# Expert rows of a sparse transformer block: stored by token through a scatter instead of by slot

## The reference, cut to what matters

```python
def hier_moe(h, ...):                       # h: (1024 tokens, 1024)
    ...                                     # group by softmax, then top 2 of its 8 experts
    experts = grp[:, None] * EXPERTS_PER_GROUP + top_i          # 2 experts a token
    dest = pstarts[e_s] + (jnp.arange(A) - starts[e_s])         # slots, padded to 128 an expert
    x_buf = zeros((P, D)).at[dest].set(tok[t_s])
    def run(xb, e):
        return (silu(xb @ w_gate[e]) * (xb @ w_up[e])) @ w_down[e]
    out = zeros((N, D)).at[t_buf].add(y_buf * w_buf[:, None])
x = x + gt2 * hier_moe(h, ...)
return rmsnorm(x, g_norm_final)
```

## Time and profile before

| what | value |
|---|---|
| median of 3 runs | 1641.82 us (1639.29 to 1643.68) |
| the profiled execution's own time | 1644.57 us |
| its span, first to last instruction | 1642.6 us |
| PE, DVE, ACT, POOL busy | 89%, 69%, 55%, 16% of the span |
| mean granted PE clock | 0.941 |
| stores of Y, `y_dram<-WK` on ACT's queue | 32 of 512 KB |
| clearing, `y_dram<-zero` on ACT's queue | 8 of 3072 KB |
| row gathers, `WK<-xn_dram,gidx` on POOL | 32 |
| last gathers, `BIG<-y_dram,srow` on POOL | 16 |

### The profile page before, as it was taken

One profiled execution on the slowest core, in us unless ns is written; L12 is line 12 of the kernel. 1 busy time (PEld: TensorE's weight loads), 2 busy tenths in 40 slices (PEclk: granted clock), 3 DMA queues, 4 the chain that ended last, 5 costly groups with the idle time before them and its releaser, 6 DMA issues.

```text
span 1642.6 us, 21585 instructions
## 1 busy us (share of the span) xinstructions
PE 1463.9 (89%) x7420; PEld 1137.6 (69%) x7420; DVE 1125.4 (69%) x1511; ACT 908.8 (55%) x1223; POOL 265.0 (16%) x191
## 2 busy tenths in 40 slices
PE   3899999999999899788899965999999999999960
PEld 2587345888887787455666654888888888888850
DVE  6632698672247994433444366999999999999947
ACT  5321577878995111423444414777777777777732
POOL 0000110240001001200000001332232232232105
PEclk9899899999999989589999986999999999999985
DMA  9198643213234233311111117999999999999957
GB/s 370 63 338 316 213 157 110 88 69 111 105 117 132 67 128 134 120 51 65 65 57 47 45 52 265 378 396 404 406 400 398 397 396 396 399 399 398 393 212 303
DMA packets 102566, 368.01 MB, mean 224 GB/s; under 512 B 11232, under 2 KB 23648, under 8 KB 77792
## 3 DMA queue, kind: packets, MB, share of 16 engines
q1 hardware_dynamic: 74208, 291.58, 46.6%
q10 hardware_dynamic: 17024, 41.95, 6.7%
q0 software_dynamic: 11264, 33.57, 5.5%
HBM read 306.24 MB, written 69.21 MB: 229 GB/s over the span
## 4 chain that ended last, share of the span: by engine, by line
PE 74%; DVE 14%; ACT 4%; issue 3%; DMA 2%; POOL 2%; SPq 0%; DVEq 0%; POOLq 0%; ACTq 0%
PE PS L1633 19%; PE PS L1635 19%; PE PS L1634 19%; PE PS L1734 3%; PE PS L1757 2%; PE PS L1956 2%; PE PS L1844 2%; PE PS L1831 1%; DVE wlo L1486 1%; DVE WK L1045 1%; DMA WK<-in_w_ada 1%; PE PS L1690 1%; POOL BIG L731 1%; PE PS L1719 1%; PE PS L1931 1%
## 5 line engine op out<-in xcount | busy, mean ns | idle before, releaser
L1486 DVE TENSOR_TENSOR wlo<-raw,whi 128x2048 fp32r<-128x2048 f32 x192 | 436.2, 2287 | 37.9 <-ACT whi L956 35.0
L956 ACT ACTIVATE whi<-raw 128x2048 fp32r<-128x2048 f32 x192 | 364.0, 1913 | 126.6 <-DVE WK L1569 80.8
L1633 PE MATMUL PS<-whi,xhi 128*128 128x512 f32 x512 | 203.9, 398 | 4.4 <-DVE xlo L1556 3.2
L1635 PE MATMUL PS<-whi,xlo 128*128 128x512 f32 x512 | 201.1, 393 | 0.0
L1634 PE MATMUL PS<-wlo,xhi 128*128 128x512 f32 x512 | 200.1, 391 | 0.0
L838 ACT ACTIVATE KV<-ACC,WK 128x1024 int8<-128x1024 f32 (+4 forms) x160 | 147.5, 925 | 23.8 <-DVE WK L1181 21.1
L1633 PE MATMUL PS<-KVR,BIGR 128*128 128x512 f32 x320 | 126.9, 397 | 1.1 <-ACT WK L823 1.1
L1635 PE MATMUL PS<-KVR,BIGR 128*128 128x512 f32 x320 | 124.9, 390 | 0.0
L1634 PE MATMUL PS<-KVR,BIGR 128*128 128x512 f32 x320 | 124.5, 389 | 0.0
L695 POOL COPY wcol<-tw 128x1 f32 (+1 forms) x32 | 63.0, 1970 | 370.1 <-DVE WK L1587 370.1
L1633 PEld LDWEIGHTS PS<-whi,xhi 128*128 128x128 f32 x512 | 97.0, 189 | 24.7 <-DVE xlo L1556 4.0
(11 more groups left out here) (329 smaller groups left out, 2907.3 us busy)
## 6 DMA issues: line engine op xcount, KB each, us to landing
raw<-in_w_gate SPq DMA_DIRECT2D x64, 1024.0 KB, 7.1
raw<-in_w_up SPq DMA_DIRECT2D x64, 1024.0 KB, 7.8
raw<-in_w_down SPq DMA_DIRECT2D x64, 1024.0 KB, 7.3
y_dram<-zero ACTq DMA_DIRECT2D x8, 3072.0 KB, 11.3
WK<-in_w_ada POOLq DMA_DIRECT2D x16, 1024.0 KB, 7.4
y_dram<-WK ACTq DMA_DIRECT2D x32, 512.0 KB, 7.1
KV<-in_w_in SPq DMA_DIRECT2D x5, 2048.0 KB, 10.2
KV<-in_x SPq DMA_DIRECT2D x16, 512.0 KB, 4.9
```

What stands on the lines that cost most here:

```text
L956: nc.scalar.activation(whi[:, slot], raw[:, q], ACT.Copy).then_inc(G("m_hi"), 1)
L1486: V.tensor_tensor(wlo[:, slot], raw[:, q], whi[:, slot].bitcast(F32), ALU.subtract)\
L1633: mm(out_, x_hi, w_hi, start=first, stop=False)
L1635: return mm(out_, x_lo, w_hi, start=False, stop=final)
```

## The change

`y_dram` becomes 2048 rows: row t holds the result of token t from one of its experts, row 1024 + t that of the other. The half is chosen in routing: the pair with the higher slot number of a token's two goes to the upper half (`at`). The table now holds the destination row (token, or 1024 + token), and serves for both directions: `xn_dram` is stored twice, one copy behind the other, so that gathering by it works too. The store from ACT is gone; POOL scatters Y by an indirect DMA that skips empty slots, one item later in its own program. The clearing is gone. At the end SP loads both halves with plain DMAs. The lower rows (y1) are complete when the last item but one has been scattered (`m_end` 1), so their loads run beside the last item's down product; DVE adds them after the last Y, and the upper rows (y2) after that. The remainder of the first gate half is made after the table instead of before it, and in the last step the remainders of the down halves are made before `h`.

```diff
-        xn_dram = nc.dram_tensor("xn_dram", (S, D), F32).ap()
-        y_dram = nc.dram_tensor("y_dram", (MAX_ITEMS * P, D), F32).ap()
+        xn_dram = nc.dram_tensor("xn_dram", (2 * S, D), F32).ap()
+        y_dram = nc.dram_tensor("y_dram", (2 * S, D), F32).ap()
...
@@ sync
-                    sp.dma_start(xn_dram[tile(TILES[i - 1]), :], WC["sq"]).then_inc(G("st_xn"), 16)
+                    for half in range(2):
+                        sp.dma_start(xn_dram[tile(T * half + TILES[i - 1]), :], WC["sq"]).then_inc(G("st_xn"), 16)
...
             sp.wait_ge(G("m_end"), 1)
-            sp.dma_start(WF["x"][T - 1], x1_dram[tile(T - 1), :]).then_inc(G(f"ld_x{T - 1}"), 16)
+            for t in range(T):
+                sp.dma_start(WF["y1"][t], y_dram[tile(t), :]).then_inc(G(f"f_y{t}"), 16)
+            sp.wait_ge(G("m_end"), 2)
+            sp.wait_ge(G("st_y1"), 8 * count(rounds))
+            for t in range(T):
+                sp.wait_ge(G(f"f_y{t}"), 16)
+                sp.dma_start(WF["y2"][t], y_dram[tile(T + t), :]).then_inc(G(f"f_y{t}"), 16)
...
@@ gpsimd
+            def scatter(s):
+                nc.gpsimd.indirect_dma_start(
+                    out=y_dram, out_offset=bass.IndirectOffsetOnAxis(ap=gidx[:, 2 + s:3 + s], axis=0),
+                    in_=WM["Y"][:, s], in_offset=None,
+                    bounds_check=2 * S - 1, oob_is_err=False).then_inc(G(f"st_y{s}"), 16)
...
                 if not last:
-                    pool.wait_ge(G("m_idx"), i + 2)
+                    pool.wait_ge(G("m_idx"), 2 * i + 2)
...
                     take_weight(i + 1, 1 - s)
+                else:
+                    pool.wait_ge(G("m_idx"), 2 * i + 2)
+
+                if not known(i, 2):
+                    pool.wait_ge(G(f"st_y{s}"), 8 * (i - s))
+                if not known(i, 1):
+                    pool.wait_ge(G("m_yd"), i)
+                take_index(tbl[:, i:i + 1] if known(i, PEELED) else tbl[:, bass.ds(i, 1)], 2 + s)
+                if not known(i, 1):
+                    scatter(1 - s)
 
             steps(pool, lambda: rounds, step)
-
-            pool.wait_ge(G("m_end"), 1)
+            pool.wait_ge(G("m_end"), 2)
+            scatter(1)
...
@@ scalar
-                if u % 2 == 0:
-                    zero_rows(u // 2)
...
-                if not known(i, 1):
-                    store(i - 1, 1 - s)
...
+            act.wait_ge(G("m_lo"), place(count(rounds) - 1, 1, UP[1])[0] + 1)
+            act.wait_ge(G("st_y0"), 8 * count(rounds))
+            act.wait_ge(G("st_y1"), 8 * count(rounds) - 16)
+            own(A(small[:, 62:63], expo[:, 0:1], ACT.Copy), G("m_end"))
             high_hidden(count(rounds) - 1)
-            store(count(rounds) - 1, 1)
...
@@ vector
+            at = WR["at"]
+            for e in range(2):
+                own.go(V.tensor_tensor(at[:, e], WR["row"][:, e], WR["row"][:, 1 - e], ALU.is_gt))
+            own.wait()
+            own(V.scalar_tensor_tensor(at, at, float(S), c("token").unsqueeze(1).to_broadcast([P, 2, T]), ALU.mult, ALU.add))
...
-            for e in range(2):
-                own(V.tensor_copy(srow[:, e, :], WR["row"][:, e]))
-            low(0, 0, GATE[0])
...
+            low(0, 0, GATE[0])
...
+            for t in range(T):
+                dve.wait_ge(G(f"ld_x{t}"), 32)
+                dve.wait_ge(G(f"f_y{t}"), 16)
+                own.go(V.tensor_tensor(WF["x"][t], WF["x"][t], WF["y1"][t], ALU.add))
+            dve.wait_ge(G("m_end"), 2)
...
             for t in range(T):
-                xf, y1, y2 = WF["x"][t], WF["y1"][t], WF["y2"][t]
+                xf = WF["x"][t]
                 dve.wait_ge(G(f"f_y{t}"), 32)
-                own(V.tensor_tensor(y1, y1, y2, ALU.add))
-                dve.wait_ge(G(f"ld_x{t}"), 32)
-                own(V.tensor_tensor(xf, xf, y1, ALU.add), G("f_sum"))
+                own(V.tensor_tensor(xf, xf, WF["y2"][t], ALU.add), G("f_sum"))
```

More of the change, by code:

```diff
@@ L281, in block_kernel @@
                    ("row", (2, T)), ("q", (2, T)), ("r", (2, T)), ("col", (1,)), ("place", (1,)), ("it", (MAX_ITEMS * NE,)),
-                   ("ef", (64,)), ("h", (64,))])
+                   ("ef", (64,)), ("h", (64,)), ("at", (2, T))])
         WR["ohp"] = WK[:, 6312:6312 + 16 * P].rearrange("p (r n) -> p r n", r=16)
@@ L287, in block_kernel @@
         NF = 4
-        WF = {name: [BIG[:, D * (T * n + t):D * (T * n + t + 1)] for t in range(T)] for n, name in enumerate(("y1", "y2"))}
+        WF = {name: [BIG[:, a + D * n:a + D * n + D] for a in places for n in range(T // 2)]
+              for name, places in (("y1", (0, 8192)), ("y2", (4096, 12288)))}
         WF["sq"] = BIG[:, 16 * D:17 * D]
         WF["x"] = [WK[:, 6312 + D * s:6312 + D * (s + 1)] for s in range(2)] + \
-            [WK[:, 1024:2048]] + [KV[:, a:a + D] for a in (4096, 6144, 7168, 8192)] + [BIG[:, 17 * D:18 * D]]
+            [WK[:, 1024:2048]] + [KV[:, a:a + D] for a in (4096, 6144, 7168, 8192)] + [WM["Xg"][:, 0]]
         WF["gf"] = WK[:, 8360:8360 + D]
         sw = sb("sw", [P, 2, T])
-        srow = sb("srow", [P, 2, T], I32)
         tbl = sb("tbl", [P, TBL], I32)
@@ L581, in _ @@
             sp.wait_ge(G("c_xn"), T + 1)
-            sp.dma_start(xn_dram[tile(TILES[T - 1]), :], WC["sq"]).then_inc(G("st_xn"), 16)
+            for half in range(2):
+                sp.dma_start(xn_dram[tile(T * half + TILES[T - 1]), :], WC["sq"]).then_inc(G("st_xn"), 16)
             sp.wait_ge(G("st_x1"), 16 * T)
@@ L621, in _ @@
             sp.wait_ge(G("r_done"), 1)
-            for t in range(T - 1):
+            for t in range(T):
+                if t == T - 1:
+                    sp.wait_ge(G("m_xtr"), count(rounds))
                 sp.dma_start(WF["x"][t], x1_dram[tile(t), :]).then_inc(G(f"ld_x{t}"), 16)
@@ L681, in _ @@
             pool.wait_ge(G("r_done"), 1)
-            pool.wait_ge(G("st_xn"), 16 * T)
+            pool.wait_ge(G("st_xn"), 32 * T)
             def take_index(column, s):
@@ L690, in gather @@
                     in_offset=bass.IndirectOffsetOnAxis(ap=gidx[:, s:s + 1], axis=0),
-                    bounds_check=S - 1, oob_is_err=False).then_inc(G(f"ld_rows{s}"), 16)
+                    bounds_check=2 * S - 1, oob_is_err=False).then_inc(G(f"ld_rows{s}"), 16)
+            def scatter(s):
[3 more added lines that the diff above has]
+                    bounds_check=2 * S - 1, oob_is_err=False).then_inc(G(f"st_y{s}"), 16)
             def take_weight(i, s):
@@ L727, in f_root @@
                 own(tt(f_rs[t], f_ms[t], expo[:, 0:1], ALU.pow), G("norm_rs"))
[L729 to L733, removed]
             for t in range(T):
@@ L759, in _ @@
             act.wait_ge(G("pool_set"), 1)
[L761 to L767, removed]
             def split_high(n, part=None):
@@ L932, in _ @@
                     if i >= 1:
-                        act.wait_ge(G("st_xn"), 16 * i)
+                        act.wait_ge(G("st_xn"), 32 * i)
                         act.wait_ge(G("c_htr"), i)
@@ L961, in high_rows @@
                     .then_inc(G("m_xhi"), 1)
[L963 to L966, removed]
             def high_hidden(i):
@@ L997, in _ @@
             steps(act, lambda: rounds, step)
+            act.wait_ge(G("m_lo"), place(count(rounds) - 1, 1, UP[1])[0] + 1)
+            act.wait_ge(G("st_y0"), 8 * count(rounds))
+            act.wait_ge(G("st_y1"), 8 * count(rounds) - 16)
+            own(A(small[:, 62:63], expo[:, 0:1], ACT.Copy), G("m_end"))
             high_hidden(count(rounds) - 1)
-            store(count(rounds) - 1, 1)
-            act.wait_ge(G("m_idx"), count(rounds) + 1)
-            act.wait_ge(G("st_y0"), 8 * count(rounds) + 64)
-            act.wait_ge(G("st_y1"), 8 * count(rounds) + 64)
+            act.wait_ge(G("m_idx"), 2 * count(rounds) + 1)
+            act.wait_ge(G("m_yd"), count(rounds))
             own(A(small[:, 62:63], expo[:, 0:1], ACT.Copy), G("m_end"))
@@ L1461, in _ @@
                             dve.wait_ge(G("c_htr"), i)
-                            dve.wait_ge(G("st_xn"), 16 * i)
+                            dve.wait_ge(G("st_xn"), 32 * i)
                     part = slice(512 * h, 512 * h + 512)
@@ L1522, in _ @@
             own(V.scalar_tensor_tensor(r16, q16, -float(P), row16, ALU.mult, ALU.add))
+            at = WR["at"]
[3 more added lines that the diff above has]
+            own(V.scalar_tensor_tensor(at, at, float(S), c("token").unsqueeze(1).to_broadcast([P, 2, T]), ALU.mult, ALU.add))
             dve.wait_ge(G("st_x1"), 16 * T)
-            dve.wait_ge(G("st_xn"), 16 * T)
+            dve.wait_ge(G("st_xn"), 32 * T)
             ohp, ohi = WR["ohp"], WR["ohi"]
@@ L1531, in _ @@
                 own.go(V.tensor_tensor(ohi[:, some, 0], ohi[:, some, 1],
-                                       c("token").unsqueeze(2).to_broadcast([P, T, TBL]), ALU.mult))
+                                       at[:, e].unsqueeze(2).to_broadcast([P, T, TBL]), ALU.mult))
```

(20 more changed lines are left out.)

## The result

The changed kernel takes 1940.62 us (median of 4 runs, 1937.75 to 1941.01) against 1642.75 before: ratio 1.1804, 95% interval 1.179 to 1.1818, 298 us slower. Forecast was 1864, range 1750 to 1945; rival B had 1945.

What follows compares the result with a forecast made beforehand. The expert stage was taken as PE-bound. 29 turns x 8.0 = 232 us, +1.3 start, -1 clearing, -10 end give +222 on 1644.57, that is 1866.9, or 1864 as median; range 1750 to 1945.

Steps and rivals of the forecast that it cites:

- rival B: Loop: the DMA queue does not drain, landing stays at 7.8; 10.8 us an item, 313 us, 1945 us; chance 17%.
- The signs named ahead: Profile after: PE waits 4 to 8 us at some 29 turns, items 22 to 28 us apart, DMA about 280 GB/s.
- the old item: Loop: the item whose down product ends at 1307.0; the following step's gather stands behind its Y, which ends at 1311.03.
- From Y to the end of the gather's issue: POOL in the loop: copy, scatter, copy, gather, held by DVE remainders; Y ends at 1311.03, the gather's issue at 1319.10.
- Rival D: Loop: DVE holds only copies, not indirect DMAs; gather ends 1.84 us earlier, 180 us in all, 1811 us; chance 5%.
- The landing: Loop: gathered rows land 5.0 us after the issue's end, as the pause drains the DMA queue; ends 3.1 and 7.8.
- The stall: PE at each turn in the loop: starts at 1324.2 instead of 1318.46, 5.7 us late; ends 3.8 and 8.5.
- The clock: PE after each stall: granted clock at half on the turn and down product, 2.3 us lost for each stall.
- Start: First gather: the first gate remainder, now behind the table, holds POOL's issue; +1.3 us, bounds 0 and +3.
- End: After the loop: POOL's 16.7 us of gathers go, DVE ends last; -10 us, between -6 and -13.
- The clearing: Beside the first projections: removing 24 MB of clearing, where PE waited 2.4 us for a late weight load; -1 us taken.

Runs made afterwards that it cites:

- experiment 1: Changed kernel with the scatter one step later in POOL's program (step i scatters item i-2): 1637.26 us, ratio 0.9966 to the kernel before.
- experiment 2: Changed kernel with the next index copy moved behind the gather, so POOL does copy, scatter, gather after Y: 1881.54 us, ratio 1.1448.
- experiment 5: Kernel of experiment 1 with the first gate remainder of item 0 moved behind the first gather and weight copy: 1635.46 us, ratio 0.995.
- experiment 3: Changed kernel loading only half of each weight tile from the third item on, same instructions on the engines: 1863.49 us, ratio 1.1342.
- experiment 4: Changed kernel with 32 extra matmuls on spare data per item, right ahead of the turn that waits for its rows: 1886.52 us, ratio 1.1479.
- experiment 8: Kernel of experiment 1 plus the 24 MB of clearing, from the same place but into a spare DRAM tensor: 1638.12 us, ratio 0.9973.

## Why the prediction was right, and where its size was off

The direction, the place and the mechanism came as forecast; the size did not. The forecast itself, 1864, missed by 77 us, and the measured 1940.62 is in the stated range only because its upper end was set at rival B, which had a chance of 17%. The signs named ahead miss the same way: waits of 8.3 us where 4 to 8 were named, items 28.3 us apart where 22 to 28 were, 247 GB/s where about 280 was.

- That PE bounds the loop, and that bytes saved give nothing: right (experiment 1, PE 200 of 200 us at 385 GB/s).
- The new order on POOL, which puts the next gather behind Y of the old item: right in place and in count, 29 turns, and it is the whole loss (experiment 1).
- From Y to the end of the gather's issue: 8.1 us worked out, 8.2 measured, with each copy and issue held as stated. Rival D falls. The Trainium skill ("SBUF — State Buffer", "Who interferes with whom"), weighed in the prediction, infers that a two-input DVE operation does not hold descriptor generation. Here the issue of the gather is held: it took 2.92 us in the loop, 2.23 where less of the remainder was left (experiment 2) and 1.16 at the start with no remainder beside it (experiment 5), and the measurement decides. Which part of the issue is held, the reading of its indices or the making of descriptors, no run here shows.
- The landing: this term was mis-sized. I took 5.0 us after the issue's end, since the pause lets the DMA queue drain; it measured 7.7. The queue does drain, but not then: DVE frees the down buffers just before the gather and the up buffers just behind it. SP issues the down loads between 1420.2 and 1422.8, ahead of the end of the gather's issue (1423.16), and the first up load at 1425.2, so the loads of both stand in the window in which the gather waits (DMA share 1.01 at 1425.5 to 1427.0, and 0 before, at 1407.7 to 1410.0). With half the bytes it landed in 4.7 (experiment 3). Rival B had the right size by that, 1945. The stall was 8.3 instead of 5.7.
- The clock: 2.3 taken; 2.1 by difference, 1.9 by experiment 4.
- Start: +1.3 taken, +2.8 measured: the issue was held as said, and the rows then also took 5.7 us from its end instead of 4.0, likely behind a weight load that the same remainder had freed (experiment 5; argued from the order of the issues).
- End: -10 taken; -12.1 after the last Y and +2.5 ahead of it make -9.6. The clearing: -1 taken, no effect found (experiment 8); a wait in the same stretch was taken for its effect.
- The sum of these: 29 x 10.47 + 2.8 - 9.6 = 297 against 222 predicted; the 2.6 us of the stall in 29 items make 76 us.

## What to carry to other kernels

On an engine that works in order, a moved operation is priced by what stands behind its wait, not by its own duration: 1.0 us of scatter cost 10.5 us an item, and one step of delay made it free. Price the landing of a small DMA by the transfers that the same moment frees, not by the mean share of the DMA engines. And a pause of PE like these (8 us) is paid a second time, about 2 us in half clock at its end, where what follows is on the loop's chain.

## What was not expected of the hardware

A gather of half-filled tiles landed 3.0 to 5.7 us after its issue's end at the start. In the loop it took 4.7 with half the weight bytes (mean DMA share 0.47), 7.7 with all of them at a share of 0.67, and in experiment 1, at a share of 0.99, again 7.4 (10.4 less 2.98). So from 0.67 to 0.99 the mean share said nothing on the landing.
